# Delta rule's input projection: two tiles from x without its norm, and the gate stages one tile later

## The chip, the cores and the metric

One core of one Trainium2 chip runs the whole program. The time is device time in microseconds (us) of one launch, inputs and outputs in HBM; several executions are taken and their median is quoted. The engines are TensorE (PE, matmul), VectorE (DVE), ScalarE (ACT), GpSimd (POOL), and SyncE (SP), whose queue starts the DMA transfers.

## What is computed

Two blocks on 256 tokens of width 1024. The first ends in a convolutional feed-forward and an RMS norm; the second puts 16 learned meta tokens ahead (272 tokens) and begins with a gated delta rule. The change lies where they meet:

```python
def _rms_norm(x, g):
    xf = x.astype(jnp.float32)
    y = xf * lax.rsqrt(jnp.mean(xf * xf, axis=-1, keepdims=True) + EPS)
    return (y * g.astype(jnp.float32)).astype(x.dtype)

x = x + g2x * _conv_ffn(hx2, rows, ...)      # its last product is "down0"
x = _rms_norm(x, final_norm_g)
h = concat([meta, x])                        # 16 + 256 tokens

proj = h @ w_in                              # q, k, v, z and the 16 gate columns b_raw, a_raw
qkv = jax.nn.silu(causal_dwconv(qkv, conv_w))          # width 4
beta = jax.nn.sigmoid(b_raw)
g = -jnp.exp(a_log) * jax.nn.softplus(a_raw + dt_bias)
g = jnp.cumsum(g, axis=-1)
decay = jnp.exp(jnp.where(causal, g[..., :, None] - g[..., None, :], -jnp.inf))
```

The norm multiplies row by row of a token: with r the reciprocal root of the token, y = r (x g), and so a product of y with the weights is r times the product of x g with them. The meta tokens have no root.

## The kernel before

**Layout.** Activations lie with the features on the 128 partitions, 8 groups (k) of 128 features, and the tokens along the free side. A weight unit is 128 output columns over all 8 k, 512 KB. Every float32 product is three matmuls in a rounded format: weights and activation are each split in a rounded part (hi) and a rest (lo), and hi hi, hi lo and lo hi are added in PSUM. A tile of 128 output columns is thus 24 matmuls of 272 columns (256 in the first block) and goes into PSUM bank (tile mod 4).

**A weight unit's way.** SP starts its DMA into one of four `w_raw` slots once GpSimd is done with the slot's last unit (`lo_ready`); ScalarE rounds it to `w_hi` (line 1689 is the helper through which all of ScalarE's operations go; `rounded(p)` in the delta-rule stage); GpSimd subtracts to `w_lo` (line 673); TensorE multiplies and raises `unit_used`, which frees the slot of `w_hi` and `w_lo`. The bank of a tile is free when `banks_free` has counted its reader. Lines 567 to 595 are SP's list, down0's 24 units (three for each of 8 tiles) in a loop and behind them eight kinds of small loads: meta tokens, mask levels, gate weights `wba`, `sel`, `pick`, `a_log`, `dt_bias`.

**Order on each engine.** It is written out by hand. At the end of the first block TensorE does down0 (line 898), the rms sums (lines 1003 and 1006: the sum of the squares of groups 0 to 6 that VectorE has built, and two more squares), the mask stage (1540 to 1543), `fill(6)` (line 739, products of the identity that nobody reads), then `a_in` (the projection, 32 tiles): tiles 0 and 1 side by side (`begin`, lines 724 to 729), each k-step with the three matmuls of the 16 gate columns beside it (`ba`, line 1535), and then tile by tile (line 763).

Their operand comes from a chain, called S_H here: ScalarE's `root` of the sums, VectorE's reciprocal (line 3119), and for each k VectorE x times `final_g` times the reciprocal root (3124), ScalarE's rounding to `a_hi` and its copy to `h`, VectorE's rest `a_lo` (3127).

**The gates.** When `ba` is done ScalarE copies `tok` and, with VectorE (3314 to 3326), forms softplus and the running sum `gcum`; ScalarE then makes the row operands (`rows_r`, `tok`, `glsp`; `rows_ready`). TensorE turns them over (`token_rows`, line 1360, and line 1550), spreads them (`broadcast_g`, line 1325, banks 4 to 7) and later `broadcast_g0` (line 1333, bank 4, once VectorE has read the two pieces of chunk 2 from it). VectorE's `differences(1)`, `(2)`, `(0)` (line 3172) read these banks. Between them lie the convolution's taps: `tap3(p)` on ScalarE multiplies tile p out of its bank with one tap, `taps(p)` on VectorE (line 3150) adds the three others from the bank, and only then is bank p mod 4 free for tile p + 4. `rounded(0)`, the rounding of unit 4, needs tile 0's slot, and so on.

Of the kernel before, what the change touches and what calls it, by code (L numbers as in the profile page):

```python
# [17 lines left out]
F32 = mybir.dt.float32  # L18
# [5 lines left out]
ds = bass.ds  # L24
# [65 lines left out]
def bass_two_blocks(nc, a, out):  # L90
    ctx = ExitStack()
    with ctx:
# [3 lines left out]
        def at(name, shape, offset, dt=F32):  # L96
            return nc.alloc_sbuf_tensor_at(name, shape, dt, offset=offset)
# [113 lines left out]
        off = arena + 47872  # L211
        cbuf = at("cbuf", [P, 4, N2], off)
# [157 lines left out]
        WBA_ROUNDED, META_ROUNDED = 1, 2  # L370
# [4 lines left out]
        S_X, S_GU, S_O, S_MERGED, S_N, S_F, S_H, S_ON, S_LN0, S_LN1, S_U, S_LN2 = range(12)  # L375
# [58 lines left out]

        def end_normed(k):

            return banks[2 + k % 2][:, 0:N1]
# [87 lines left out]
        def _(sp):  # L525
            def small(dst, src, s):
                sp.dma_start(dst, src).then_inc(s, 16)
# [39 lines left out]
            for name, parts in STREAMS:  # L567
                if parts is None:
                    with sp.Fori(0, 2) as it:
                        for j in range(4):  # L570
                            for b, (k0, kn) in enumerate(DOWN_SPLIT):
                                n = 3 * j + b
                                sp.wait_ge(lo_ready, it * 12 + (u0 + n - 3))
                                unit_src = a[name][ds(it * 4 + j, 1), :, k0:k0 + kn] \
                                    .rearrange("o p k m -> (o p) k m")
                                sp.dma_start(w_raw[:, n % 4, 0:kn], unit_src).then_inc(landed[n % 4], 16)
                    if name == "down0":
                        sp.wait_ge(split_ready, 8 * S_F + 8)
                        sp.wait_ge(unit_used, UNIT0["up0"] + 2)
                        small(h[:, :, 0:META], a["meta"], stage_in)  # L580
                        small(levels[:], a["levels"], gdn_in)
                        sp.wait_ge(cleared, 2)
                        small(wba[:, :, 0:HN], a["w_ba"][:, :, HN:], gdn_in)
                        small(wba[:, :, 32:], a["w_ba"][:, :, 0:HN], gdn_in)
                        small(sel_both[0:HN], a["sel"], gdn_in)
                        small(sel_both[32:32 + HN], a["sel"], gdn_in)
                        small(pick[:], a["pick"], gdn_in)
                        small(hb[:, 0:1], a["a_log"], gdn_in)
                        small(hb[:, 1:2], a["dt_bias"], gdn_in)
                    u0 += 24  # L590
                    continue
# [111 lines left out]
        def _(pe):  # L703
# [30 lines left out]

            def fill(n):


                for _ in range(n):
                    mm(banks[7][:, 384:512], ident[:], ident[:], start=True, stop=True)
# [545 lines left out]
            rms(RMS_END)  # L1285
# [21 lines left out]
            def a_in(first, last):  # L1307
                lin("a_in", N2, whole2, tiles=(first, last), first=Z0 if first >= 24 else 0)
# [230 lines left out]
            pe.wait_ge(gdn_in, 128)  # L1539
            mm(banks[7][:, 256:384], ident[:], ident[:], start=True, stop=False)  # L1540
            for lv in range(4):
                mm(banks[7][:, 256:384], levels[:, lv], ident[:], start=False, stop=(lv == 3))
            nc.tensor.transpose(banks[4][:, 0:P], levels[:, FIRST], ident[:]).then_inc(stage_done, 1)
            fill(6)
            lin("a_in", N2, whole2, S_H, tiles=(0, 2), beside=ba, together=2)
            pe.wait_ge(h_kept, KD)
            a_in(2, 5)
# [3 lines left out]
            a_in(5, 6)  # L1551
            broadcast_g()
            a_in(6, 8)
# [125 lines left out]
        def _(act):  # L1679
# [396 lines left out]
            end_square = square_after("down0")  # L2076
            down(0, end_square, (0, 1))
            u0 = UNIT0["down0"]
            for n in range(12, 24):
                act.wait_ge(unit_used, u0 + n + 1)  # L2080
                if n == 23:
                    end_square(7)
                round_unit(u0 + n + 4, n % SLOTS)
                if n % 3 == 2 and n < 23:
                    end_square(n // 3)
                if n == 18:
                    act.wait_ge(gdn_in, 128)
                    fn(wba_hi[:], wba[:], ACT.Copy).then_inc(wba_rounded, 1)
                    act.wait_ge(stage_in, 80)
                    fn(a2_hi[:, :, 0:META], h[:, :, 0:META], ACT.Copy).then_inc(wba_rounded, 1)  # L2090
# [11 lines left out]
            def tap3(p):  # L2102

                act.wait_ge(unit_used, u0 + p + 1)
                if p == 16:
                    act.wait_ge(stage_done, DONE["hq"])
                w = PV["a_conv"] + 3 * 24 + A_ORDER[p]
                fn(region(p), banks[p % SLOTS][:, 0:N2], ACT.Copy, scale=pv[:, w:w + 1]).then_inc(conv_evac, 1)
# [64 lines left out]

            nc.scalar.preload_act_table_set("natural_log_exp_and_others")
            tap3(0)
            act.wait_ge(gdn_in, 128)
            fn(sel_r[:], sel_both[:], ACT.Copy)
# [7 lines left out]
            rounded(0)  # L2185
            tap3(1)
            rounded(1)
# [6 lines left out]
            act.sem_inc(taken[7], 1)  # L2194
            act.wait_ge(gcum_ready, 1)
# [9 lines left out]
            rounded(2)  # L2205
            tap3(3)
            rounded(3)
# [414 lines left out]
        def _(dve):  # L2622
# [330 lines left out]

            def residual(i, name, j):

                def take(t, s):
                    tile = down_bank(0, s)
                    if product_halves(t):
                        link(v.scalar_tensor_tensor(x[:, t], tile[:, N1:], mod[:, 0, t + j * KD:t + j * KD + 1], x[:, t],
                                                    ALU.mult, ALU.add))  # L2960
                    v.scalar_tensor_tensor(x[:, t], tile[:, 0:N1], mod[:, 0, t + j * KD:t + j * KD + 1], x[:, t],
                                           ALU.mult, ALU.add).then_inc(banks_free, 1)
                    if s < 3:
                        dve.wait_ge(sq_ready, t + (8 * i + 1))
                        dve.wait_ge(part_seq, t + (9 * (i - RMS_F) + 1))
                        v.tensor_tensor(part_sum[:, 0:N1] if t == KD - 2 else grown_end, grown_end, sq[:, t, 0:N1], ALU.add) \
                            .then_inc(part_seq, 2 if s == 2 else 1)

                v.memset(grown_end, 0.0).then_inc(part_seq, 1)
                return take  # L2970
# [59 lines left out]
            def ffn(i, n, taps, first=0):  # L3030
# [54 lines left out]
                for p in range(4):  # L3085
                    step(p, p)
                pairs(dve, 4, KF, step)
# [25 lines left out]
            v.memset(sel_both[:], 0.0)  # L3113
            v.memset(wba[:], 0.0).then_inc(cleared, 1)
# [4 lines left out]
            link(v.reciprocal(r_end, r_end))  # L3119
            for k in range(KD + 1):  # L3120
# [186 lines left out]

            link(v.memset(tokm[:], 1.0))
# [3 lines left out]
            taps(0)  # L3312
# [20 lines left out]
            taps(1, 2, 3)  # L3333
# [689 lines left out]
```

## Time and profile before

| | |
|---|---|
| median of 3 runs | 1247.93 us (1247.92 to 1249.58) |
| profiled execution | 1246.66 us, its span 1244.9 us |
| mean granted TensorE clock | 0.996 |
| TensorE busy | 1222.6 us, 98% |
| GpSimd | 880.4 us, 71% |
| VectorE | 737.0 us, 59% |
| ScalarE | 722.2 us, 58% |

The profile is one execution; its times run from the start of the span. A row of a timeline gives a start, the time from it to the end of the group, engine, line, operation, what is written and read, the count, and in brackets the idle time before it with what ended it. Matmuls are pipelined, so a duration of 0.29 stands at a distance of 0.125 from start to start. A float32 matmul of `rms`, the masks and `fill` has two records.

### The profile page before, as it was taken

To read this page: it belongs to the slowest core of one execution; us is meant where nothing else is said; L and a number is where in the kernel's file an instruction comes from. 1 tells how busy PE (TensorE), PEld (TensorE's weight loads), DVE (VectorE), ACT (ScalarE), POOL (GpSimd) and SP (SyncE) were. 2 spreads that over 40 slices of the span, in tenths; PEclk is the share of its full clock that TensorE was granted. 3 is DMA by queue.
4 is the path that set the end of the run, shared out by engine and by line. 5 is a ranking of instruction groups with operands and counts; after the bars stand their busy time and mean duration, and the time that the engine had idled before them with its cause. 6 is when DMAs were issued, how large, how long until landed. Compare 5 with 4: busy or idle time off the path is not lost.

```text
span 1244.9 us, 26168 instructions
## 1 busy us (share of the span) xinstructions
PE 1222.6 (98%) x9026; PEld 1126.5 (90%) x9026; DVE 737.0 (59%) x1719; ACT 722.2 (58%) x1325; POOL 880.4 (71%) x387
## 2 busy tenths in 40 slices
PE   9999999999999999999999999999999999999997
PEld 4688899988998898899899999999999999999986
DVE  3989972244587774169884475555534757555633
ACT  3656654565666665479643276666655547666743
POOL 0357957568869888858532158888888868888795
PEclk9999999999999999999999999999999999999999
DMA  9995355446647665745332136555566655655562
GB/s 371 407 363 186 101 187 153 121 150 202 184 144 214 185 181 174 200 132 166 115 93 69 52 103 188 183 174 177 163 180 187 175 164 172 198 175 183 156 194 72
DMA packets 66037, 217.75 MB, mean 175 GB/s; under 512 B 9904, under 2 KB 17328, under 8 KB 62624
## 3 DMA queue, kind: packets, MB, share of 16 engines
q1 hardware_dynamic: 65952, 216.59, 55.6%
q8 instruction: 57, 0.93, 0.3%
q14 instruction: 28, 0.23, 0.1%
HBM read 215.52 MB, written 1.05 MB: 174 GB/s over the span
## 4 chain that ended last, share of the span: by engine, by line
POOL 38%; issue 37%; PE 22%; ACT 1%; POOLq 1%; DVE 1%; ACTq 0%; DVEq 0%
POOL w_lo L673 37%; PE bank L802 10%; PE bank L1135 5%; PE bank L894 3%; PE bank L903 1%; PE bank L898 1%; POOL w_lo L680 1%; POOLq L670 0%; ACT h L1689 0%; POOLq L672 0%; ACT w_hi L1689 0%; PE bank L724 0%; PE bank L948 0%; PE bank L729 0%; PE bank L725 0%
## 5 line engine op out<-in xcount | busy, mean ns | idle before, releaser
L673 POOL TENSOR_TENSOR w_lo<-w_raw,w_hi 128x1024 fp32r<-128x1024 f32 x340 | 812.9, 2405 | 326.7 <-ACT w_hi L1689 325.5
L1689 ACT ACTIVATE w_hi<-w_raw 128x1024 fp32r<-128x1024 f32 (+1 forms) x372 | 378.0, 1020 | 104.4 <-PE bank L903 39.5
L802 PE MATMUL bank<-a_hi,w_hi 128*128 128x264 f32 (+3 forms) x704 | 200.4, 285 | 0.1
L802 PE MATMUL bank<-a_hi,w_lo 128*128 128x264 f32 (+3 forms) x704 | 200.2, 284 | 0.0
L802 PE MATMUL bank<-a_lo,w_hi 128*128 128x264 f32 (+3 forms) x704 | 199.9, 284 | 0.0
L802 PEld LDWEIGHTS bank<-a_hi,w_hi 128*128 128x128 f32 x704 | 132.8, 189 | 0.4 <-DVE a_lo L3662 0.3
L802 PEld LDWEIGHTS bank<-a_lo,w_hi 128*128 128x128 f32 x704 | 132.9, 189 | 0.1
L802 PEld LDWEIGHTS bank<-a_hi,w_lo 128*128 128x128 f32 x704 | 132.9, 189 | 0.0
L3736 DVE SCALAR_TENSOR_TENSOR bank<-row_mean,cols,bank 128x260 f32<-128x260 f32 (+3 forms) x112 | 54.7, 488 | 117.1 <-ACT cols L1689 112.7
L763 PE MATMUL bank<-a_parts,w_hi 128*128 128x256 f32 x448 | 81.5, 284 | 0.5 <-DVE a_parts L2948 0.4
L894 PE MATMUL bank<-g_parts,w_hi 128*128 128x512 f32 x308 | 79.1, 397 | 0.7 <-DVEq L3838 0.7
L680 POOL TENSOR_TENSOR w_lo<-w_raw,w_hi x32 | 58.0, 1843 | 23.9 <-ACT w_hi L1689 23.1
L3038 DVE SCALAR_TENSOR_TENSOR cbuf<-bank,pv,cbuf 128x189 f32<-128x189 f32 (+2 forms) x176 | 65.6, 423 | 14.4 <-ACT cbuf L1689 13.9
L763 PE MATMUL bank<-a_hi,w_hi 128*128 128x272 f32 (+1 forms) x240 | 71.5, 298 | 0.4 <-POOL w_lo L673 0.4
L763 PEld LDWEIGHTS bank<-a_parts,w_hi 128*128 128x128 f32 x448 | 69.9, 192 | 1.2 <-DVE a_parts L2948 0.6
L763 PE MATMUL bank<-a_hi,w_lo 128*128 128x272 f32 (+1 forms) x240 | 69.7, 290 | 0.0
L763 PE MATMUL bank<-a_lo,w_hi 128*128 128x272 f32 (+1 forms) x240 | 69.7, 290 | 0.0
L894 PEld LDWEIGHTS bank<-g_parts,w_hi 128*128 128x128 f32 x308 | 54.9, 188 | 11.1 <-DVEq L3838 0.9
L931 PE MATMUL bank<-g_parts,w_hi 128*128 128x260 f32 x352 | 64.0, 284 | 0.7 <-DVEq L3838 0.7
L785 PE MATMUL bank<-a_parts,w_hi 128*128 128x512 f32 x256 | 64.3, 393 | 0.3 <-ACTq L1963 0.3
L808 PE MATMUL bank<-a_parts,w_hi 128*128 128x512 f32 x256 | 64.1, 392 | 0.0
L763 PE MATMUL bank<-a_parts,w_lo 128*128 128x256 f32 x224 | 63.4, 283 | 0.0
(548 smaller groups left out, 2931.1 us busy)
## 6 DMA issues: line engine op xcount, KB each, us to landing
w_raw<-in_s SPq DMA_DIRECT2D x284, 512.0 KB, 3.6
w_raw<-in_down SPq DMA_DIRECT2D x48, 512.0 KB, 3.6
adaw<-in_w_ada SPq DMA_DIRECT2D x16, 1024.0 KB, 9.9
w_raw<-in_down SPq DMA_DIRECT2D x24, 384.0 KB, 3.2
adab<-in_w_ada_first SPq DMA_DIRECT2D x8, 1024.0 KB, 8.2
ctxt<-in_ctx SPq DMA_DIRECT2D x1, 1024.0 KB, 11.2
x<-in_x SPq DMA_DIRECT2D x1, 1024.0 KB, 15.1
out_h<-h SPq DMA_DIRECT2D x4, 256.0 KB, 2.6
```

The costliest lines, as they stand in the source:

```text
L673: pool.tensor_tensor(w_lo[:, s], w_raw[:, s], w_hi[:, s].bitcast(F32), ALU.subtract) \
L680: pool.tensor_tensor(w_lo[:, :, ds(k, 1)], w_raw[:, :, ds(k, 1)], w_hi[:, :, ds(k, 1)].bitcast(F32), ALU.subtract) \
L763: ins = mm(banks[s][:, first:n], w_[:, s, k], x_[:, k, first:n], start=(m == 0), stop=(m == 3 * KD - 1))
L785: mm(banks[s][:, :].rearrange("p (two n) -> p two n", two=2), w_hi[:, s, k], a_parts[:, :, k, cols], start=(k == 0), stop=False)
L802: ins = mm(banks[bank][:, tk], w_[:, s, k], x_[:, k, tk], start=(m == 0), stop=(m == 3 * KD - 1))
L808: mm(banks[bank][:, :].rearrange("p (two n) -> p two n", two=2), w_hi[:, s, k], a_parts[:, :, k, N1:], start=(k == 0), stop=False)
L894: mm(dst[:, :].rearrange("p (two n) -> p two n", two=2), w_hi[:, s, k], g_parts[:, :, kk, first:n], start=(kk == 0), stop=False)
L931: ins = mm(banks[t][:, first:N2], w_[:, s, k], x_[:, k0 + k, first:N2], start=(m == 0), stop=(m == 3 * KF - 1))
L1135: ins = mm(banks[b][:, :].rearrange("p (u m) -> p u m", u=SLOTS), x_[:, k, tk], w_[:, :, k], start=(k == 0 and i == 0), stop=(k == KD - 1 ...
L1689: return nc.scalar.activation(out_, in_, f, **kw)
L3038: v.scalar_tensor_tensor(dst, frm(banks[banks_of(p)[0]][:, 0:n]), pv[:, ds(pair + w, 1)], dst, ALU.mult, ALU.add).then_inc(conv_seq, 1)
L3736: return v.scalar_tensor_tensor(dst, row_mean[:, N2 - dst.shape[-1]:], by, dst, ALU.mult, ALU.add)
```

## The change

New side operands `nx_hi` and `nx_lo` hold x times the learned column (`final_g`), rounded and rest, with the meta tokens ahead. They are made tile by tile within down0, ScalarE's rounding behind its square, VectorE's rest behind its residual. The last x tile is built in a free half of PSUM bank 3 and copied from there. TensorE does tiles 0 and 1 from these operands, with `rms` behind the first k-step and the masks behind the second; VectorE multiplies tiles 0 and 1 by the reciprocal root in PSUM (`TILE0_SCALED`, `TILE1_SCALED`) and ScalarE's `tap3(0)` and `tap3(1)` wait for that. Tiles 2 and 3 are done side by side from the normed operand, with `ba` beside them. `fill(6)` and the wait for `h_kept` are gone. The row stage stands behind tile 5 in place of 4, `broadcast_g` behind 6 in place of 5; `broadcast_g0` stays behind 7. ScalarE's and VectorE's lists follow; the normed groups use other banks, and VectorE waits for the masks before them. Of the small loads the meta tokens, levels and gate weights move ahead of down0, the rest between its halves.

```diff
@@ SP @@
+                        sp.wait_ge(cleared, 2)
                         small(h[:, :, 0:META], a["meta"], stage_in)
                         small(levels[:], a["levels"], gdn_in)
-                        sp.wait_ge(cleared, 2)
                         small(wba[:, :, 0:HN], a["w_ba"][:, :, HN:], gdn_in)
                         small(wba[:, :, 32:], a["w_ba"][:, :, 0:HN], gdn_in)
+                        down_units(0, 1)
                         small(sel_both[0:HN], a["sel"], gdn_in)
                         small(sel_both[32:32 + HN], a["sel"], gdn_in)
                         small(pick[:], a["pick"], gdn_in)
                         small(hb[:, 0:1], a["a_log"], gdn_in)
                         small(hb[:, 1:2], a["dt_bias"], gdn_in)
+                        down_units(1, 2)
@@ TensorE @@
-            rms(RMS_END)
+            def side_by_side(tiles, ops, split, beside, first=1):
+                u0, t0 = UNIT0["a_in"], TILE0["a_in"]
+                for k in range(KD):
+                    pe.wait_ge(split_hi, 8 * split + max(k + 1, first))
+                    for t in tiles:
...
+                        mm(banks[t][:, 0:N2], w_hi[:, t, k], ops[0][:, k, 0:N2], start=(k == 0), stop=False)
+                        mm(banks[t][:, 0:N2], w_lo[:, t, k], ops[0][:, k, 0:N2], start=False, stop=False)
+                    pe.wait_ge(split_ready, 8 * split + max(k + 1, first))
...
+                    beside(k)
...
-            fill(6)
-            lin("a_in", N2, whole2, S_H, tiles=(0, 2), beside=ba, together=2)
-            pe.wait_ge(h_kept, KD)
-            a_in(2, 5)
+            def root_and_masks(k):
+                if k == 0:
+                    rms(RMS_END)
+                if k == 1:
...
+            side_by_side((0, 1), (nx_hi, nx_lo), S_NX, root_and_masks, first=KD - 1)
+            side_by_side((2, 3), whole2, S_H, ba)
+            a_in(4, 6)
             pe.wait_ge(rows_ready, 1)
             token_rows(7, (1, 2))
...
-            a_in(5, 6)
+            a_in(6, 7)
             broadcast_g()
-            a_in(6, 8)
+            a_in(7, 8)
             broadcast_g0()
             a_in(8, 10)
@@ ScalarE @@
+            def end_tile(t):
+                act.wait_ge(banks_free, t + (TILE0["down0"] + 5))
+                fn(sq[:, ds(t, 1), 0:N1], x[:, ds(t, 1)], ACT.Square).then_inc(sq_ready, 1)
+                fn(nx_hi[:, ds(t, 1), META:], x[:, ds(t, 1)], ACT.Copy, scale=pv[:, ds(t + PV["final_g"], 1)]).then_inc(split_hi, 1)
...
                 if n == 23:
-                    end_square(7)
+                    act.wait_ge(full_ready, LAST_X)
+                    fn(sq[:, 7, 0:N1], last_x, ACT.Square).then_inc(sq_ready, 1)
+                    fn(x[:, 7], last_x, ACT.Copy)
+                    fn(nx_hi[:, 7, META:], last_x, ACT.Copy, scale=column("final_g", 7)).then_inc(split_hi, 1)
                 round_unit(u0 + n + 4, n % SLOTS)
@@ VectorE @@
+            def scaled_x_rest(t, src):
+                dve.wait_ge(split_hi, 8 * S_NX + t + 1)
+                v.scalar_tensor_tensor(nx_lo[:, t, META:], src, col("final_g", t), nx_hi[:, t, META:].bitcast(F32),
+                                       ALU.mult, ALU.subtract).then_inc(split_ready, 1)
...
             link(v.reciprocal(r_end, r_end))
+            dve.wait_ge(stage_done, DONE["masks"])
...
+            link(v.tensor_copy(rstd[:, 0:N1], r_end))
+            for t in range(2):
+                dve.wait_ge(unit_used, UNIT0["a_in"] + t + 1)
+                tile = banks[t][:, META:N2]
+                v.tensor_tensor(tile, tile, rstd[:, 0:N1], ALU.mult).then_inc(full_ready, 1)
...
-            taps(0)
+            taps(0, 1)
...
-            taps(1, 2, 3)
+            taps(2, 3)
```

ScalarE's list behind the normed groups moves as a whole. Before, word for word in the order of the program (`kr<-bank` is a `tap3`, `w_hi<-w_raw` a rounding, `tok<-bank 8x272` the first that needs `ba`):

```order
L2174 ACT_TABLE_LOAD
L1689 ACTIVATE kr<-bank,pv 128x272
L1689 ACTIVATE sel_r<-sel 128x1024
L1689 ACTIVATE tok<-bank 8x272
...
L1689 ACTIVATE w_hi<-w_raw 128x1024
L1689 ACTIVATE kr<-bank,pv 128x272
L1689 ACTIVATE w_hi<-w_raw 128x1024
L1689 ACTIVATE halves<-bank 64x32 x2
L1689 ACTIVATE lower_70<-bank 128x128
L1689 ACTIVATE rows_r<-bank 8x272
```

ScalarE in the changed kernel, the same place:

```order
L1716 ACTIVATE w_hi<-w_raw 128x1024 x2
L2215 ACT_TABLE_LOAD
L1716 ACTIVATE kr<-bank,pv 128x272 x2
L1716 ACTIVATE tok<-bank 8x272
...
L1716 ACTIVATE w_hi<-w_raw 128x1024
L1716 ACTIVATE halves<-bank 64x32 x2
L1716 ACTIVATE lower_70<-bank 128x128
L1716 ACTIVATE w_hi<-w_raw 128x1024
L1716 ACTIVATE sel_r<-sel 128x1024
L1716 ACTIVATE rows_r<-bank 8x272
```

Two roundings and the second `tap3` moved ahead of `tok`, the two later roundings and `sel_r` stand between `tok` and the row operands.

TensorE around the row stage before, with the bank numbers (the row stage writes bank 7, the tile behind it bank 1):

```order
L763 MATMUL bank0<-a2_hi_144,w_lo_51 128x272
L1360 MATMUL bank7<-ident_53,tok_189 16x8 x2
L1360 MATMUL bank7<-ident_53,tok_189 128x8 x4
L1550 MATMUL bank7<-glsp_193,averages_54 128x8
L763 MATMUL bank1<-a2_hi_144,w_hi_50 128x272
```

The same place on TensorE in the changed kernel:

```order
L768 MATMUL bank1<-a2_hi_146,w_lo_51 128x272
L1382 MATMUL bank7<-ident_53,tok_191 16x8 x2
L1382 MATMUL bank7<-ident_53,tok_191 128x8 x4
L1577 MATMUL bank7<-glsp_195,averages_54 128x8
L768 MATMUL bank2<-a2_hi_146,w_hi_50 128x272
```

The tile behind the row stage is now tile 6, in bank 2, which held tile 2; before it was tile 5, in bank 1.

## Rows read from the trace of the kernel before

**Rows 1.** The page: busy time, share and instructions of each engine.

```profile
PE 1222.6 (98%) x9026; PEld 1126.5 (90%) x9026; DVE 737.0 (59%) x1719; ACT 722.2 (58%) x1325; POOL 880.4 (71%) x387
```

**Rows 2.** Timeline of TensorE (start, duration, engine, line, operation, count, idle before): projection's start.

```profile
534.83 0.59 PE L1003 MATMUL bank<-part_sum,averages 128*128 128x256 f32 x2
...
536.07 0.70 PE L1006 MATMUL bank<-sq,averages 128*128 128x256 f32 x2 [0.22 <-ACT sq L1689]
...
537.83 1.50 PE L739 MATMUL bank<-ident 128*128 128x128 f32 x12
540.19 0.36 PE L724 MATMUL bank<-a_hi,w_hi 128*128 128x272 f32 x1 [0.85 <-ACT a_hi L1689]
```

**Rows 3.** Timeline of TensorE, tile 2 to the second gate stage.

```profile
549.49 0.29 PE L763 MATMUL bank<-a_hi,w_hi 128*128 128x272 f32 x1
...
559.33 0.45 PE L1360 MATMUL bank<-ident,tok 8*16 8x8 f32 x6
...
559.93 0.39 PE L763 MATMUL bank<-a_hi,w_hi 128*128 128x272 f32 x1
...
563.04 1.11 PE L1325 MATMUL bank<-rows_r,sel_r 128*128 128x256 f32 x8
...
570.13 0.56 PE L1333 MATMUL bank<-tok,sel_r 8*16 8x16 f32 x16
```

**Rows 4.** Timeline of ScalarE in the gate stages.

```profile
549.57 1.05 ACT L1689 ACTIVATE sel_r<-sel 128x1024 fp32r<-128x1024 f32 x1
550.63 0.39 ACT L1689 ACTIVATE tok<-bank 8x272 f32<-8x272 f32 x1
...
552.53 1.04 ACT L1689 ACTIVATE w_hi<-w_raw 128x1024 fp32r<-128x1024 f32 x1
553.47 0.46 ACT L1689 ACTIVATE kr<-bank,pv 128x272 f32<-128x272 f32 x1
...
555.59 0.39 ACT L1689 ACTIVATE rows_r<-bank 8x272 fp32r<-8x272 f32 x1
...
557.50 0.46 ACT L1689 ACTIVATE kr<-bank,pv 128x272 f32<-128x272 f32 x1
```

**Rows 5.** Timeline of VectorE in the gate stages.

```profile
557.14 4.52 DVE L3150 SCALAR_TENSOR_TENSOR kr<-bank,pv,kr 128x269 f32<-128x269 f32 x9
...
564.19 2.16 DVE L3172 SCALAR_TENSOR_TENSOR dd<-bank,toks,levels 128x128 f32<-128x128 f32 x8 [0.17 <-PE bank L1325]
...
569.46 2.15 DVE L3172 SCALAR_TENSOR_TENSOR dd<-bank,toks,levels 128x128 f32<-128x128 f32 x8
```

**Rows 6.** Timeline of VectorE in down0 and at its end.

```profile
511.79 0.48 DVE L2959 SCALAR_TENSOR_TENSOR x<-bank,mod,x 128x256 f32<-128x256 f32 x1 [6.72 <-PE bank L903]
...
519.51 0.48 DVE L2959 SCALAR_TENSOR_TENSOR x<-bank,mod,x 128x256 f32<-128x256 f32 x1 [5.80 <-PE bank L903]
...
535.43 1.26 DVE L3117 TENSOR_TENSOR a_lo<-h,a_hi 128x128 fp32r<-128x128 f32 x1
```

**Rows 7.** Timeline of GpSimd in down0 and behind it.

```profile
480.54 37.77 POOL L673 TENSOR_TENSOR w_lo<-w_raw,w_hi 128x1024 fp32r<-128x1024 f32 x16 [3.80 <-ACT w_hi L1689]
...
531.80 9.42 POOL L673 TENSOR_TENSOR w_lo<-w_raw,w_hi 128x1024 fp32r<-128x1024 f32 x4
```

**Rows 8.** Timeline of the DMA queue: down0's end to a_in's units.

```profile
519.06 0.66 SPq L527 DMA_DIRECT2D h<-in_meta  x1
...
521.96 2.24 SPq L527 DMA_DIRECT2D sel<-in_sel  x2
...
525.73 15.99 SPq L530 DMA_DIRECT2D w_raw<-in_s  x8
```

**Rows 9.** Windows, delta-rule stage: us, PE busy, PEld, DVE, ACT, POOL; then PEclk.

```profile
667.00:670.00 3.00, 2.69 (x37) 2.40 (x35) 2.21 (x4) 0.76 (x2) 1.02 (x1) 0.92 0.22 53
670.00:673.00 3.00, 3.00 (x16) 3.00 (x15) 0.00 (x1) 0.00 (x0) 0.00 (x0) 0.51 0.32 127
```

**Rows 10.** Timeline of TensorE ahead of those windows.

```profile
664.15 1.92 PE L1480 MATMUL bank<-vb,uu 16*16 16x128 f32 x16
```

## What the change will do to the time

> **What bounds the kernel now.** I read the page first: TensorE is busy for 1222.6 us of the span of 1244.9 [rows 1]. So a us on TensorE's path counts whole, and a us elsewhere counts only if TensorE comes to wait for it. The second reading is TensorE's timeline where the projection `a_in` begins. Behind down0's last matmul stand the rms sums from 534.83, the masks, then twelve records of `fill` from 537.83 (1.50 us), a wait of 0.85 us for the first operand, and tile 0 at 540.19 [rows 2]. Between 534.83 and 540.19 there are 5.36 us without a projection matmul. The third reading is the gate stages. TensorE shows no gap there [rows 3], and that misleads. VectorE is as tight: between its taps at 557.14, the differences of chunk 1 at 564.19 and those of chunk 2 at 569.46 it pauses once, for 0.17 us, for TensorE's broadcast [rows 5]. Then TensorE's `g0` stage, which needs a bank that the second differences give back, starts at 570.13, 0.67 us after they start [rows 3, 5]. So from 564 on two engines run in step, and a delay of either is a delay of both. This decides the case.
>
> **The front, TensorE.** Tiles 0 and 1 no longer need the root, so their first k-step starts at 534.83 in place of the rms. A k-step of two tiles is 6 matmuls. The old 72 matmuls of the first group took 540.19 to 549.49, 9.30 us or 0.129 each with the restart in it; 24 of a tile with a restart took 559.93 to 563.04, 3.11 us [rows 2, 3]. Without a restart I take 0.127, so 48 are 6.1 us. The rms and the masks still stand between them: 534.83 to 537.83 less the 0.22 of wait, 2.8 us, and the wait goes because 0.75 us of matmuls now lie ahead of them [rows 2]. Tiles 2 and 3 with `ba` start at 534.83 + 6.1 + 2.8 = 543.7. Their operand is there: it came at 540.19 before [rows 2] and the chain behind it is late only by what ScalarE adds ahead of the root (a copy and the last `nx_hi`, about 0.4 each by the 0.4 us ones of [rows 4]), near 541. They are 72 matmuls, 9.1 us, up to 552.8. Before, two tiles and `ba` were done at 549.49 and the third tile would have ended 3.0 us on, at 552.5, the fourth at 555.5; now four are done at 552.8. TensorE is **2.7 us ahead**. This is 1.50 of fill, 0.85 and 0.22 of waits, and rounding.
>
> **What moves the other way: the gates.** `ba` is done at 552.8 instead of 549.49. Its result reaches ScalarE some 0.15 after the next matmul starts, 552.9. ScalarE came to it at 550.63 before, since the rounding of `sel_r` (549.57, 1.06) stood ahead [rows 4]. That is 2.3 us later. Behind it on ScalarE, from `tok` to the taps of tile 2, stood 550.63 to 557.50, 6.87 us [rows 4]. Of that list tap3(1) leaves (0.46 long by its row at 553.47, and 0.4 of path, since neighbours overlap a little) and `sel_r` with 1.06 comes in; both roundings stay. So tap3(2) starts at 552.9 + 6.87 - 0.4 + 1.06 = 560.4, against 557.50.
>
> **Who waits for that.** After the two side-by-side groups TensorE does tiles 4 and 5 (6.1 us, to 558.9), then stands at the row stage, whose operand ScalarE finishes some 0.2 before tap3(2), at 560.2: a wait of 1.3. The row stage is 559.33 to 559.93, 0.6 [rows 3], to 560.8. Next is tile 6, which goes into bank 2, where tile 2 lies until VectorE's three taps have read it. They start with tap3(2)'s result at 560.4 + 0.5 and take a third of the 4.52 of three tiles [rows 5], 1.5, so bank 2 is free at 562.4: a second wait, 1.6. Tile 6 takes 3.1, and `broadcast_g` starts at 565.5 against 563.04 [rows 3]. VectorE begins the differences 1.15 after it (563.04 to 564.19 [rows 3, 5]), at 566.65. That is **+2.46 us** against 564.19. From there VectorE has the same list as before; chunk 2's differences come 5.27 later, the `g0` stage at 572.6, while TensorE with tile 7 would be there at 569.6 and waits the 3.0 that it was ahead. From `g0` on both engines carry the +2.46, and no later TensorE wait that I find is against an engine that did not shift too.
>
> **Edits that I cost at nothing.** SP: the small loads that stood behind down0 took 519.06 to 525.73, and now 2.9 us of them stand ahead of down0 and 3.8 (521.96 to 525.73) between its halves [rows 8]. GpSimd subtracts 16 units without a gap in 37.77 us, 2.36 per unit, and SP issues a unit at that pace; 3.8 in place of a 2.4 pause makes one unit 1.4 late. With that cover gone it would cost up to 1.4. VectorE's eight `nx_lo` and ScalarE's eight `nx_hi` stand in the 7.72 us of a down0 tile (511.79 to 519.51 [rows 6]), of which VectorE uses less than 2. VectorE's two scalings of PSUM tiles (0.48 each by the rows of its PSUM operations [rows 6]) come after its normalisation chain and ahead of taps(0), which is early. GpSimd is done with the first units of `a_in` at 541.2 (end of the four of [rows 7]), before tile 2 starts in either kernel.
>
> **A rule weighed.** The subtraction of the meta columns, two SBUF inputs, took 1.26 us from 535.43 to 536.69 while GpSimd's second unit of that run ended at 531.80 + 4.71 = 536.51 [rows 6, 7]: it sat until GpSimd's operation was over, then ran in under 0.2. The change adds eight operations of this kind in down0 (seven `nx_lo` and the meta one). If each also holds GpSimd back by its own 0.4, GpSimd's three units per tile go from 7.08 to 7.5, still under TensorE's 7.72 [rows 6, 7]. The Trainium skill, SBUF — State Buffer, section "Who interferes with whom", says that a VectorE instruction with two SBUF inputs and a GpSimd instruction that reads SBUF exclude each other for the whole instruction. By that rule the sum gains nothing; it would gain if the margin of 0.2 per tile were used up.
>
> **Rivals.** (1) **The lead is kept**: if the gates' results are not what ends last, tile 6 follows tile 5 and the broadcast, and VectorE, come early. Even then VectorE has the cumulative sum (ScalarE's 1.9 and as much again), taps of two tiles (3.0) and a broadcast ahead, so differences at 562 at the earliest, 2.2 to 2.7 before 564.19: 1247.93 - 2.7 = 1245.2. Against it: bank 2. (2) **Half way**: TensorE's lead is lost and the delay is absorbed, by the small pauses of VectorE and a shorter ScalarE list than I add up: 0 to +1.5, 1248.7. (3) **Slower still**: one mechanism, GpSimd in down0. If the margin of 0.2 us per tile is overrun, by 0.2 to 0.4 over seven tiles, TensorE waits 1.4 to 2.8 for `w_lo` in down0 and all that follows is later: 1247.93 + 2.5 + 1.5 = 1251.9, at most 1253.2. It decides from 0.2 us per `nx_lo` more than I allow. (4) **The clock.** The granted clock fell to 0.92 and 0.51 in the two windows from 667 to 673, that is to 1.2 GHz, after a run of small matmuls that began at 664.15 [rows 9, 10]; this costs 0.24 + 1.47 = 1.7 us. The change puts waits of 1.3, 1.6 and 3.0 us within 14 us. If they bring one more such fall, 1250.4 + 1.7 = 1252.1; if the shift takes the old one away, 1248.7. The Trainium skill, TensorE: Matmul & The Clock Gate, section "What's actually happening", has the array's clock halve when the engine was not busy enough; the rows at 667 agree. (5) **It does not do what it says**: were `nx` late, tile 0 would still wait near 540 and no lead arise; the gates would be 2.7 later again, 1253.
>
> **How the numbers follow.** The profiled execution is 1246.66 us, so this one would be 1249.1; the median of the three runs is 1247.93 and I put the difference on that: 1247.93 + 2.46 = **1250.4**. Chances: forecast (+1.9 to +3.0) 0.50; rival 1 0.09; rival 2 with the lost clock fall 0.18; rivals 3 and 5 0.13; one more clock fall 0.10. About 0.2% or 2.5 us is what a measurement of this kernel can tell from no change; the forecast lies on that line, so its 0.50 splits 0.27 to 0.23. Same: 0.27 + 0.18 + 0.01 = 0.46. Slower: 0.23 + 0.13 + 0.10 = 0.46. Faster: 0.08. The range leaves out most of rival 1 and the far end of rival 3: 1246.4 to 1252.8.
>
> **What would show it.** Right: tile 0 of `a_in` starts within 0.2 of down0's end; tile 2 near 543.7; TensorE waits at the row stage, at tile 6 for VectorE, and about 3 us at `g0`; the differences of chunk 1 start 2.5 later. Wrong: `ba` early, tile 6 without a wait, or new waits for `w_lo` inside down0.

## The result and the profile after

The changed kernel takes 1252.83 us (1251.42 to 1254.35, 7 runs), the kernel before in the same comparison 1249.18 us (1247.33 to 1250.17, 7 runs). The ratio is 1.0034, with a 95% interval of 1.0025 to 1.0044: slower by 3.1 to 5.5 us. A ratio here and below comes from the single executions of both kernels, and is not the quotient of the two medians, which are 3.65 us apart. The profiled execution is one with 1253.29 us; its span is 1251.5 us against 1244.9, and its mean granted clock 0.991 against 0.996. All seven executions of the changed kernel have 0.990 to 0.994.

The page's first line of the changed kernel, to set beside [rows 1]:

```profile
PE 1226.0 (98%) x9014; PEld 1130.1 (90%) x9014; DVE 749.0 (60%) x1731; ACT 725.5 (58%) x1335; POOL 881.4 (70%) x387
```

TensorE has twelve records fewer (the fill) and is busy 3.4 us longer. That is the first hint: fewer matmuls took more time. The front of the projection came as announced. TensorE of the changed kernel from the end of down0, which answers to [rows 2] (columns as there):

```profile
534.89 0.28 PE L903 MATMUL bank<-g_parts,w_lo 128*128 128x256 f32 x1
535.01 0.29 PE L1300 MATMUL bank<-nx_hi,w_hi 128*128 128x272 f32 x1
...
535.77 0.59 PE L1008 MATMUL bank<-part_sum,averages 128*128 128x256 f32 x2
```

Tile 0 starts 0.12 after down0's last matmul, where before the rms sums, the masks, the fill and a wait lay. The rms sums now stand behind the first k-step, without a wait. Next the three longest waits of TensorE from 534 to 600 (releaser, sum, times, longest); a fourth, of 0.2, was there before too:

```profile
PE bank L1355 <- DVE dd L3229: 2.9, 1, 2.9
PE bank L768 <- DVE kr L3207: 1.7, 1, 1.7
PE bank L1382 <- ACT glsp L1716: 1.3, 1, 1.3
```

They are the three that the prediction had: the row stage (1.3 forecast), bank 2 (1.6), `g0` (3.0). The rows with their starts, of ScalarE, TensorE and VectorE, against [rows 3 to 5]:

```profile
552.78 0.39 ACT L1716 ACTIVATE tok<-bank 8x272 f32<-8x272 f32 x1 [1.66 <-PE bank L1557]
...
560.27 0.83 ACT L1716 ACTIVATE kr<-bank,pv 128x272 f32<-128x272 f32 x2
```

```profile
560.10 0.45 PE L1382 MATMUL bank<-ident,tok 8*16 8x8 f32 x6 [1.29 <-ACT glsp L1716]
...
562.48 0.36 PE L768 MATMUL bank<-a_hi,w_hi 128*128 128x272 f32 x1 [1.71 <-DVE kr L3207]
...
564.00 0.43 PE L768 MATMUL bank<-a_hi,w_hi 128*128 128x272 f32 x1
...
567.09 1.11 PE L1347 MATMUL bank<-rows_r,sel_r 128*128 128x256 f32 x8
...
574.16 0.60 PE L1355 MATMUL bank<-tok,sel_r 8*16 8x16 f32 x16 [2.91 <-DVE dd L3229]
```

```profile
568.24 2.16 DVE L3229 SCALAR_TENSOR_TENSOR dd<-bank,toks,levels 128x128 f32<-128x128 f32 x8 [3.55 <-PE bank L1347]
```

Tile 6 starts at 562.48, 2.55 later than the tile in that place before (559.93), as forecast; 0.18 of this was already there at the end of down0. Then it takes 4.61 us to the broadcast instead of 3.11: from the seventh of its 24 matmuls (563.32) until 566.5 they start 0.23 apart, not 0.125. The windows of the changed kernel (us, PE busy and records, granted clock, DMA share, GB/s) say why:

```profile
562.00:564.00 2.00, 1.52 (x9) 0.82 0.62 240
564.00:566.00 2.00, 2.00 (x10) 0.50 0.00 0
566.00:568.00 2.00, 2.00 (x16) 0.83 0.00 0
...
570.00:572.00 2.00, 1.24 (x10) 1.00 0.62 234
572.00:574.00 2.00, 0.00 (x0) 0.88 0.57 145
574.00:576.00 2.00, 1.84 (x22) 0.50 0.29 117
576.00:578.00 2.00, 2.00 (x10) 0.50 0.14 14
578.00:580.00 2.00, 2.00 (x11) 0.50 0.76 246
580.00:582.00 2.00, 2.00 (x17) 0.92 0.72 225
```

The clock fell twice to 1.2 GHz (0.50 of 2.4): once behind the waits of 1.29 and 1.71 us and once behind the one of 2.91. In the kernel before every window from 560 to 582 has 1.00. A window at half clock shows a fully busy engine with 10 to 12 matmuls in 2 us, where at full clock there are 18. The shift of TensorE against the kernel before tells the price of each part: 2.55 at tile 6, 4.05 at the broadcast (563.04 to 567.09), 4.03 at `g0` and 6.57 from the `hk` stage on (576.86 to 583.43) and to the end. So in this profile 2.5 us are the gates' path, 1.5 the first fall and 2.5 the second.

One more fall is instructive since it costs nothing. At the second block's next stage TensorE waited 1.56 us before (until 723.96, for VectorE's `a_lo`), and no fall followed. In the changed kernel the clock fell just ahead of this wait, which shrank to 0.2, and the shift stayed at 6.6:

```profile
726.00:728.00 2.00, 2.00 (x14) 0.78 0.00 0
728.00:730.00 2.00, 2.00 (x12) 0.50 0.00 0
```

Not every fall stands behind a wait: ahead of this one lie 13 small matmuls of 8 rows (724.27 to 725.81), and the last wait above 0.3 us ended at 720.16. What brought it stays open.

### The profile page after: what moved, and what is told of

The parts are those of the page before. It is cut to its first block, busy times and chain, and to the rows that moved or that the text cites. A ratio compares the mean times of both kernels' runs of the same rounds, so it can differ in the third digit from the quotient of the medians.

```text
span 1251.5 us, 26101 instructions
## 1 busy us (share of the span) xinstructions
PE 1226.0 (98%) x9014; PEld 1130.1 (90%) x9014; DVE 749.0 (60%) x1731; ACT 725.5 (58%) x1335; POOL 881.4 (70%) x387
## 4 chain that ended last, share of the span: by engine, by line
POOL 38%; issue 37%; PE 22%; ACT 1%; POOLq 1%; DVE 1%; ACTq 0%; DVEq 0%
POOL w_lo L684 37%; PE bank L807 10%; PE bank L1140 5%; PE bank L899 3%; PE bank L908 1%; PE bank L903 1%; POOL w_lo L691 1%; POOLq L681 0%; ACT h L1716 0%; POOLq L683 0%; ACT w_hi L1716 0%; POOL pick L701 0%; PE bank L735 0%; PE bank L953 0%; PE bank L740 0%
```

## Experiments

The two theories left for the extra 4 us of the profile: **A**, TensorE's waits bring the two falls of the clock between 560 and 582; **B**, the falls come by chance or from the matmuls themselves. The 2.5 us below them rest on the theory of the gates' path (ScalarE's list, bank 2, VectorE). The kernel before ran again beside each group of experiments; its medians there were 1249.13, 1248.45, 1248.57 and 1247.96 us, and each ratio is to these runs (the products in tile 7 alone belong to the last group).

**Keeping TensorE busy in its waits.** Products of the identity, 0.25 us each, into unused columns of the bank of the tile being built:

```diff
+            def a_in_padded(t, n):
...
+                        if m == 3 * KD - 1:
+                            for _ in range(n):
+                                mm(banks[s][:, 384:512], ident[:], ident[:], start=False, stop=False)
...
-            a_in(4, 6)
+            a_in(4, 5)
+            a_in_padded(5, 11)
...
-            a_in(7, 8)
+            a_in_padded(7, 11)
```

> The changed kernel with eleven products of the identity (11 x 0.25 = 2.75 us) ahead of the last matmul of tile 5 and as many in tile 7, into unused columns of the tile's bank. They stand where TensorE of the changed kernel waits: 1.29 + 1.71 us behind tile 5, 2.91 us behind tile 7. Theory A, the waits bring the two falls of the clock at 563 and 574 (1.5 and 2.5 us): both falls go, TensorE waits under 0.5 us in each place, the time is 2.5 us above the kernel before, ratio 1.0020, some 4 us of the profiled execution's span less than 1251.5. Theory B, the falls come from somewhere else, by chance or by the matmuls themselves: they stay and the ratio stays at 1.0034. Theory C, the filler delays tiles 5 and 7 and something needs them: ratio above 1.0034.

Measured: 1250.12 us, ratio to the kernel before 1.0013 (1.0004 to 1.0022). Its waits from 534 to 600 and its windows there:

```profile
PE bank L768 <- DVE kr L3223: 0.6, 1, 0.6
PE bank L1370 <- DVE dd L3245: 0.5, 1, 0.5
```

```profile
560.00:564.00 4.00, 3.38 (x32) 1.00 0.70 225
564.00:568.00 4.00, 4.00 (x35) 1.00 0.02 4
568.00:572.00 4.00, 4.00 (x36) 1.00 0.46 131
572.00:576.00 4.00, 3.53 (x41) 1.00 0.47 131
576.00:580.00 4.00, 4.00 (x40) 1.00 0.68 181
```

Both falls are gone, and the shift is 2.54 at tile 6 and stays at 2.5 until 669. A fall at 670, in the delta rule's small matmuls, then takes it to 3.5; the kernel before has a shorter one there [rows 9]. TensorE does 22 matmuls more than the changed kernel that nobody reads, and the program is faster by 2.6 us (1.0034 against 1.0013, and the two intervals do not meet). The granted clock of each execution says the same: 0.994 to 0.997 in all eleven of this kernel, 0.990 to 0.994 in the seven of the changed one. Theory A stands for these two falls, B does not. The 5.5 us of filler lie in time that was waited before, since tile 6 and `g0` start no later than the gates' path has them.

The same with the products in tile 5 alone, and then in tile 7 alone:

> The changed kernel with the eleven products in tile 5 alone. Theory A: tile 6 runs at the full clock (its 24 matmuls in 3.1 us instead of 4.6), the differences of chunk 1 start 2.5 us later than before and not 4.05; the wait of 2.9 us behind tile 7 and the fall behind it stay, so the time is 1.5 us below the changed kernel's profile and 5 us above the kernel before in a profile that has the second fall. Theory B: tile 6 is slow as before.

> The changed kernel with the eleven products in tile 7 alone. Theory A (each fall follows the waits just ahead of it): tile 6 is slow as in the changed kernel (4.6 us, a fall at 563), the fall behind g0 is gone; shift to the kernel before 2.5 at tile 6, 4.05 from the broadcast on to 660; ratio 1.0025. Theory B (one fall draws the next): no difference to the changed kernel's 6.6.

With the first alone: 1252.30 us, ratio 1.0027 (1.0012 to 1.0041). Tile 6 ran at full clock (windows 560 to 568 at 1.00), the second fall stayed (0.50 from 572 to 578), the shift from `hk` on is 4.99. With the second alone: 1253.64 us, 1.0036 (1.0023 to 1.0050). The first fall stayed and lasted longer, from about 562 to 568.5 in place of 563 to 567 (shift 5.0 at the broadcast, 4.05 expected), and none followed behind `g0`:

```profile
560.00:562.00 2.00, 0.67 (x8) 0.92 0.59 209
562.00:564.00 2.00, 1.54 (x7) 0.50 0.74 246
564.00:566.00 2.00, 2.00 (x11) 0.50 0.01 4
566.00:568.00 2.00, 2.00 (x10) 0.50 0.00 0
568.00:570.00 2.00, 2.00 (x17) 0.88 0.13 18
```

So in the profiles each of the two falls follows its own waits. In time neither edit alone can be told from the changed kernel's 1.0034: the second gave 1.0036, with granted clocks of 0.991 to 0.994, where 1.0025 was expected (just inside its interval). Only both together gave a gain clear of noise. The length of a fall varies, 1.5 to 2.7 us of cost for the same waits, and this execution had another fall at 644 in the delta rule's small matmuls. Single executions of one kernel lie up to 3 us apart here (1251.42 to 1254.35), up to 6 in the kernel before (1247.29 to 1253.19); so one profile's 6.6 us is not the 3.7 of the medians or the 4.2 of the ratio.

**The other place that lost its filler.** The changed kernel removed `fill(6)` from the front. Is that safe in itself?

```diff
-            fill(6)
             lin("a_in", N2, whole2, S_H, tiles=(0, 2), beside=ba, together=2)
```

> The kernel before without its six products of the identity ahead of a_in (it leaves out no part of the result). The wait for the first operand grows from 0.85 to 2.35 us and ends at the same time, 540.19. Theory A: a wait of 2.35 us lies between the 1.7 and 2.9 us that came ahead of falls, so the clock falls in the first group and the time grows by 1.5 to 3 us, ratio 1.001 to 1.0025. Theory B: ratio 1.000, no fall between 540 and 550.

Measured: 1251.29 us, ratio 1.0016 (1.0007 to 1.0025). TensorE of this kernel, and its windows (the profiled execution, 1248.60 us, is the shortest of eleven):

```profile
540.56 0.36 PE L724 MATMUL bank<-a_hi,w_hi 128*128 128x272 f32 x1 [2.19 <-ACT a_hi L1688]
...
542.14 0.43 PE L724 MATMUL bank<-a_hi,w_hi 128*128 128x272 f32 x1
```

```profile
540.00:542.00 2.00, 1.44 (x9) 0.91 0.77 213
542.00:544.00 2.00, 2.00 (x11) 0.50 0.75 213
544.00:546.00 2.00, 2.00 (x14) 0.74 0.60 205
```

The first operand came no later than before (540.56, when down0 had ended 0.37 later), and from 541.69 on the clock was down, for 1.5 us of cost. Nothing but six matmuls whose results nobody reads was taken out, and the kernel is 2 us slower (0.9 to 3.1). The fill in the kernel before was not decoration: with 1.5 us of it and a wait of 0.85 the clock stayed at 1.00. The changed kernel could drop it since no wait is left there.

**The gates' path.** ScalarE's list, `sel_r` into its idle 1.66 us ahead of `tok`, the fourth rounding behind `tap3(3)`:

```diff
             tap3(1)
+            fn(sel_r[:], sel_both[:], ACT.Copy)
             act.wait_ge(stage_done, DONE["ba"])
...
-            rounded(3)
-            fn(sel_r[:], sel_both[:], ACT.Copy)
             act.wait_ge(gcum_ready, 1)
...
             tap3(2)
             tap3(3)
+            rounded(3)
```

> The changed kernel with ScalarE's sel_r ahead of the first operation on the gates, in its idle 1.66 us there, and the fourth rounding behind tap3(3). Theory of the gates (their path ends last): the row operands then wait for the running sum (557.40) and no longer for ScalarE, so they, tap3(2), bank 2 and the differences of chunk 1 come 0.9 us earlier, TensorE's first wait shrinks from 1.29 to 0.4; the profile is 0.9 us shorter by this alone, and by up to 1.5 more if the fall in tile 6 goes with the shorter wait. Rival (another queue holds tile 6): nothing moves.

Measured: 1251.28 us, ratio 1.0024 (1.0013 to 1.0035). ScalarE and VectorE of this kernel:

```profile
557.53 0.39 ACT L1716 ACTIVATE rows_r<-bank 8x272 fp32r<-8x272 f32 x1 [1.14 <-DVE tok L3388]
...
559.44 0.83 ACT L1716 ACTIVATE kr<-bank,pv 128x272 f32<-128x272 f32 x2
```

```profile
567.27 2.16 DVE L3229 SCALAR_TENSOR_TENSOR dd<-bank,toks,levels 128x128 f32<-128x128 f32 x8 [3.31 <-PE bank L1347]
```

The first rows now wait for VectorE's running sum, `tap3(2)` starts 0.83 earlier and the differences 0.97 earlier. TensorE's first wait is 0.4, the other two and both falls stay. The trace confirms the path, and a first wait shorter by 0.9 us did not save the clock. The ratio alone does not show it: its interval overlaps that of the changed kernel.

Order and filler together (eight products in tile 5, eleven in tile 7):

> Both edits that helped by themselves: ScalarE's order with sel_r early and the fourth rounding late, and the filler products, eight in tile 5 and eleven in tile 7. If the two causes add: differences of chunk 1 at 565.8 (1.6 us later than before), no falls at 560 and 574, ratio 1.0013 less 0.0007, that is 1.0006, and 1.6 us above before in the profile up to 660. If they do not add (the filler now holds the broadcast back): as with the filler alone, 2.5 us.

Measured: 1249.43 us, ratio 1.0012 (1.0004 to 1.0021); the trace has the differences at 565.71, 1.5 later than before, no fall from 555 to 600 and a shift of 1.3 to 1.6 up to 640. In the trace the two causes add as expected; the ratio cannot tell the expected 1.0006 from the 1.0013 of the filler alone.

**A version in which the gates come early.** If the 2.5 us are the later `ba`, then `ba` too should come from x times the column, since the root can be put on its 16 rows as on the tiles. The main edits (the lists of ScalarE and VectorE and the places of the stages move with them, as the expectation says):

```diff
-                for m, (w_, x_) in enumerate(((wba_hi, a2_hi), (wba_lo, a2_hi), (wba_hi, a2_lo))):
+                for m, (w_, x_) in enumerate(((wba_hi, nx_hi), (wba_lo, nx_hi), (wba_hi, nx_lo))):
...
+                if k == 2:
+                    pe.wait_ge(std_ready, RMS_END + 1)
+                    ba(0)
+                    ba(1)
+                if k > 1:
+                    ba(k)
...
+            gates = banks[5][0:40, META:N2]
+            v.tensor_tensor(gates, gates, rstd[0:40, 0:N1], ALU.mult).then_inc(full_ready, 1)
```

> The changed kernel with the gate columns too taken from x times the learned column: ba stands beside tiles 0 and 1 (from their third k-step on, when the root has been read out of its bank), VectorE multiplies the 16 gate rows by the root in PSUM, the row stage stands behind tile 4 and the broadcast behind tile 5 as in the kernel before, and ScalarE's list is row operands first. Theory (the gates' path from ba to the differences of chunk 1 is what set the +2.5): the first operation on the gates starts at about 549.7 instead of 552.78, the differences of chunk 1 at about 561.4 instead of 568.24 (564.19 before), TensorE waits under 1 us in each place and no fall of the clock lies between 555 and 600; time 1.5 to 3 us below the kernel before, ratio 0.998. Rival (VectorE's own list is full from 550 on and cannot start the differences earlier than 564): ratio 1.000.

Measured: 1248.75 us, ratio 1.0001 (0.9993 to 1.0010). The whole loss is gone, but there is no gain. The gates came early as expected (`tok` at 550.28, with down0's end 0.65 later than before), the first wait was 0.97, and no fall of the clock lay from 555 to 600. But `g0` waited 1.6 us, and the differences started at 563.92, not 561.4: the number that the rival had given, and its ratio. One row of VectorE shows where the time went, with GpSimd's beside it:

```profile
561.33 2.56 DVE L3420 TENSOR_TENSOR rows_r<-tok,rows_r 8x272 fp32r<-8x272 f32 x1
563.92 2.16 DVE L3236 SCALAR_TENSOR_TENSOR dd<-bank,toks,levels 128x128 f32<-128x128 f32 x8
```

```profile
558.84 4.76 POOL L684 TENSOR_TENSOR w_lo<-w_raw,w_hi 128x1024 fp32r<-128x1024 f32 x2 [2.78 <-ACT w_hi L1723]
```

An operation of 0.43 us (its twin on the first rows takes that) sat until GpSimd's second subtraction ended at 563.60. It has two SBUF inputs, as the meta subtraction of [rows 6]. In the kernel before the same operation took 1.92 us from 562.10, while GpSimd subtracted until 563.72; the broadcast ended later still, so nothing came of it. It was moved to a place where GpSimd rests; a version of it with three filler products in tile 4's wait ran beside it:

```diff
             dve.sem_inc(taken[6], 1)
+            dve.wait_ge(rows_hi, 2)
+            v.tensor_tensor(rows_r[32:32 + HN, 1], tok[:, 2], rows_r[0:HN, 1].bitcast(F32), ALU.subtract).then_inc(rows_lo, 1)
             taps(2, 3)
...
-            dve.wait_ge(rows_hi, 2)
-            v.tensor_tensor(rows_r[32:32 + HN, 1], tok[:, 2], rows_r[0:HN, 1].bitcast(F32), ALU.subtract).then_inc(rows_lo, 1)
```

> The kernel with the gates from x, and the second rest of the row operands (VectorE, tok and rows_r) moved from behind the copies of the token columns to right behind the first rest, ahead of the taps of tiles 2 and 3. In the run before it took 2.56 us from 561.33, while GpSimd's pick ran; moved, it falls in VectorE's idle 0.50 us at 557.3, with GpSimd idle. Theory (VectorE's operation with two SBUF inputs sat through GpSimd's): it takes 0.43 us, the differences of chunk 1 start at about 561.9 to 562.6 (563.92 in the run before, 564.19 in the kernel before), TensorE's wait at g0 falls from 1.6 to under 1, ratio 0.9985 to the kernel before. Rival (VectorE would have waited for the broadcast anyway, which starts at 561.39 and ends at 562.5): differences at 562.6, 1.3 us gained, ratio 0.999.

> The same with three products of the identity ahead of the last matmul of tile 4, in the wait of 0.97 us for the row operands. No fall of the clock lay there without them, so the time is that of the run beside it; if the filler matters, through the clock a little later, a fall in the delta rule's stages between 560 and 600 is missing.

Measured: 1250.26 us, 1.0004 (0.9995 to 1.0013), and 1247.81 us, 0.9996 (0.9987 to 1.0005). Neither is clear of the kernel before; the 0.9985 of the theory did not come. I had named `pick` as the operation waited for in the run before; the rows say it was the subtraction of a unit. Moved, the operation took 0.43 and the differences came at 562.3, limited by the broadcast as the rival said. Then VectorE waited for ScalarE, and TensorE's 1.5 us at `g0` remained (VectorE in the version without the filler):

```profile
562.32 2.16 DVE L3236 SCALAR_TENSOR_TENSOR dd<-bank,toks,levels 128x128 f32<-128x128 f32 x8 [1.41 <-PE bank L1348]
564.83 1.57 DVE L3214 SCALAR_TENSOR_TENSOR kr<-bank,pv,kr 128x269 f32<-128x269 f32 x3 [0.34 <-ACT kr L1723]
567.71 1.57 DVE L3214 SCALAR_TENSOR_TENSOR kr<-bank,pv,kr 128x269 f32<-128x269 f32 x3 [1.32 <-ACT kr L1723]
```

The profile without the filler had falls at 570 (behind the wait of 1.5) and at 638, the one with it had neither. Whether three products 15 us ahead did that is not settled: `g0`'s wait was the same in both, and the two intervals overlap.

The last version, built on the one with the filler, gives ScalarE the list that VectorE waits for:

```diff
             act.sem_inc(taken[7], 1)
+            fn(sel_r[:], sel_both[:], ACT.Copy).then_inc(masks_filled, 1)
             act.wait_ge(gcum_ready, 1)
...
             tap3(3)
-            fn(sel_r[:], sel_both[:], ACT.Copy).then_inc(masks_filled, 1)
             rounded(3)
+            tap3(4)
...
-            tap3(4)
+            tap3(5)
             rounded(4)
...
-            tap3(5)
```

> The kernel with the gates from x, the second rest early and three filler products, and ScalarE's list changed again: sel_r stands in ScalarE's idle 1.27 us ahead of the row operands, tap3(4) ahead of the table load, tap3(5) ahead of the fifth rounding. In the two runs before, VectorE waited 0.34 and 1.32 us for tap3(4) and tap3(5), and TensorE 1.5 us at g0 for VectorE. Theory (ScalarE's list took the gain back): both waits go, the differences of chunk 2 start at about 567.6 and g0 at 568.3 (570.13 in the kernel before), and all that follows is 1.6 to 1.9 us earlier than in the kernel before: ratio 0.9986. Rival (units: the rounding of unit 8 behind two more operations makes tile 8 wait): g0 at 568.5 and then a wait for w_lo of up to 1.5, ratio 0.9995.

Measured: **1246.62 us, ratio 0.9984 (0.9974 to 0.9993)**: faster than the kernel before by 0.9 to 3.2 us, and than the changed kernel by 6.2 us (0.9984 against 1.0034); the medians lie 1.3 us below the kernel before. Against the version before it (0.9996) the gain is not clear of noise, and the trace has to show it. TensorE and VectorE of this kernel:

```profile
568.01 0.56 PE L1371 MATMUL bank<-tok,sel_r 8*16 8x16 f32 x16
```

```profile
564.38 3.04 DVE L3229 SCALAR_TENSOR_TENSOR kr<-bank,pv,kr 128x269 f32<-128x269 f32 x6
567.34 2.15 DVE L3251 SCALAR_TENSOR_TENSOR dd<-bank,toks,levels 128x128 f32<-128x128 f32 x8
```

No wait at `g0`, which starts 2.12 us earlier than in the kernel before (570.13 in [rows 3]); the shift is -1.9 to -2.2 up to 648. In the delta rule's small matmuls its profile has a longer fall of the clock than before, from 665, which gives about 1.2 of it back; the span is 0.9 us shorter than before.

## Why the prediction was wrong, point by point

**Direction and mechanism.** The forecast was slower by 2.46 us by the gates' path, and that path is there to a tenth: `ba` seen by ScalarE at 552.78 (552.9 forecast), `tap3(2)` at 560.27 (560.4), waits of 1.29, 1.71 and 2.91 (1.3, 1.6, 3.0), tile 6 at 562.48 (562.4; down0 had ended 0.18 later). The filler experiment, which leaves this path alone, has a ratio of 1.0013 (+0.5 to +2.7 us) and a shift of 2.54 in its trace.

**The step that failed** is the sentence "Tile 6 takes 3.1, and `broadcast_g` starts at 565.5". It took 4.6 and the broadcast started at 567.09. Behind `g0` the same happened again: "both engines carry the +2.46" from there on, says the text, and TensorE carried 4.03 at `g0` and 6.57 behind it. The sum priced every matmul behind the three waits at full clock, though the text itself counted waits of 1.3, 1.6 and 3.0 us within 14 us and had the row of a fall [rows 9]. I made the clock a rival with a chance of 0.10, and one fall of 1.7. It was part of the likeliest case: two falls, 1.5 and 2.5 us in the profile, 2.6 us by the ratios of the runs with and without filler. With the falls the trace's sum is 2.55 + 1.5 + 2.5 = 6.6. The ratio's 4.2 us split in the 1.6 that stay with the filler and the 2.6 that it took away.

**What should have told me.** The kernel before held the evidence: six matmuls with no reader in front of a wait. I read them as 1.5 us to be won and asked what the wait behind them cost, not what they kept up. The kernel before without them is 2 us slower, more than the 1.5 us that they take.

**The yardstick.** The 1250.4 was put on a median of three runs, 1247.93. Over seven runs the kernel before has 1249.18, and in the later comparisons 1247.96 to 1249.13. With the 1.25 more the forecast would have been 1251.7, and the range moved up by as much would have held the result. So half of the 2.4 us between forecast and result is the yardstick. The other 1.2 us are the net of the falls (2.6 by the ratios) and of a gates' path that the ratio with filler puts at 1.6 (0.5 to 2.7) in place of 2.46. That makes 1.7, and the ratio is half a us above the medians here. The top of the range, 1252.8, lay 0.03 under the result; it held one extra fall, not two. On which side of its end the result fell was luck; that the term of the falls was missing was not.

**Costed at nothing, rightly.** Down0 ended at the same place: its last matmul starts at 534.89 against 534.71, with 0.14 of the difference already there at 20 us, so the small loads, the eight `nx` operations of each engine and the scalings cost TensorE nothing. The blocking between VectorE and GpSimd that I weighed for `nx_lo` was there, and stronger for VectorE than I allowed. VectorE of the changed kernel, two of the seven `nx_lo` that read x from SBUF, and the last, which reads PSUM:

```profile
483.29 2.50 DVE L2996 SCALAR_TENSOR_TENSOR nx_lo<-x,pv,nx_hi 128x256 fp32r<-128x256 f32 x1
...
521.59 0.54 DVE L2996 SCALAR_TENSOR_TENSOR nx_lo<-x,pv,nx_hi 128x256 fp32r<-128x256 f32 x1
...
536.86 0.48 DVE L2996 SCALAR_TENSOR_TENSOR nx_lo<-bank,pv,nx_hi 128x256 fp32r<-128x256 f32 x1 [1.15 <-ACT nx_hi L1716]
```

The seven took 0.54 to 2.62 us. The first one ended at 485.79, and GpSimd's second unit at 480.72 + 2 x 2.42 = 485.56. VectorE had the time in each down0 tile. GpSimd's 20 units behind 480.72 took 48.40 us, 2.42 each against 2.36 of [rows 7], so three take 7.3 of TensorE's 7.72. On the gates' path of my own version there was no such time to spare.

**Rivals.** The lead was not kept (bank 2, as said). The third, GpSimd in down0, did not come. The fourth, the clock, did, twice. The Trainium skill, TensorE: Matmul & The Clock Gate, section "What's actually happening", says that a clock gate halves the engine's clock when it has not been busy. I had cited it and given it too little weight; the runs with and without filler agree with it.

## What to carry to other kernels

A wait of TensorE is not worth its length alone: in these profiles its clock fell behind single waits of 2.2 and 2.9 us, and behind two of 1.3 and 1.7 close together, and took another 1.5 to 2.7 us each time. When a change turns a spread of work into waits, price the matmuls behind them at both clock levels; and before a matmul without a reader is removed, look for the wait it stands in front of. Bringing one engine ahead gains nothing while another, here VectorE behind ScalarE, hands it its next operand: a gain clear of noise came only once the gates' inputs, VectorE's blocked operation and ScalarE's order had all moved, with three filler products beside them.

## What was not expected of the hardware

Work that nobody reads made the program faster, 22 matmuls by 2.6 us, and six of them removed made it slower by 0.9 to 3.1 us. A wait of 0.85 us behind 1.5 us of fill brought no fall; one of 2.19 in the same place did. A wait of 1.5 to 1.6 at `g0` was followed by a fall in one profile and by none in two, and the 1.56 at 723.96 in the kernel before by none. A fall directly ahead of that wait was free. And a 0.43 us operation of VectorE on eight partitions took 2.56 while GpSimd subtracted a unit.
